# Expert weight rows relaid over partitions so that each partition reads 8 KB in one piece, in a hybrid decoder layer

## The reference

```python
# h: (256, 1024); 32 experts, each token uses 2 of them (gates is zero elsewhere)
def expert(acc, prm):
    wg, wu, wd, gt = prm                     # (1024, 512), (1024, 512), (512, 1024), (256,)
    hid = jax.nn.silu(h @ wg) * (h @ wu)
    return acc + gt[:, None] * (hid @ wd), None
out, _ = lax.scan(expert, jnp.zeros_like(h), (w_gate, w_up, w_down, gates.T))
```

## Time and profile before

| | us |
|---|---|
| median of 3 runs | 739.86 |
| lowest, highest of them | 738.91, 739.90 |
| span of the profiled execution | 794.1 |

### The profile page before, as it was taken

How to read it: one execution, slowest core, us unless ns; L and a number is a source line. 1 busy time by engine, 2 the same in 40 slices (tenths; PEclk the granted TensorE clock), 3 DMA queues, 4 the chain that set the end, 5 groups by cost and what they waited for, 6 DMA issues and landing times.

```text
span 794.1 us, 13163 instructions
## 1 busy us (share of the span) xinstructions
PE 771.8 (97%) x4865; PEld 590.9 (74%) x4865; DVE 647.9 (82%) x579; ACT 524.6 (66%) x577; POOL 139.2 (18%) x190
## 2 busy tenths in 40 slices
PE   6999999999799999999999999999999999999994
PEld 6774774535688888888888888888888888888873
DVE  3631759656869999999899999999899999999895
ACT  4011333544577888787887888787887888787883
POOL 5400200130231122111111122111111122111000
PEclk9988888888788888888888888888888888888887
DMA  9998966943598999999999999999999999999901
GB/s 320 352 369 319 386 241 253 360 170 118 188 321 307 357 359 352 343 355 349 358 343 355 372 343 359 335 358 359 355 335 363 349 359 352 342 358 357 323 1 56
DMA packets 102153, 249.20 MB, mean 314 GB/s; under 512 B 5265, under 2 KB 5325, under 8 KB 100077
## 3 DMA queue, kind: packets, MB, share of 16 engines
q1 hardware_dynamic: 99648, 244.33, 84.9%
q0 software_dynamic: 1008, 3.31, 1.2%
q10 hardware_dynamic: 1470, 1.22, 0.5%
HBM read 247.78 MB, written 1.07 MB: 313 GB/s over the span
## 4 chain that ended last, share of the span: by engine, by line
PE 95%; DVE 2%; DMA 1%; ACT 1%; issue 0%; SPq 0%; DVEq 0%
PE PS L1558 48%; PE PS L1546 8%; PE PS L1507 6%; PE PS L1252 4%; PE PS L1296 4%; PE PS L1525 4%; PE PS L1516 4%; PE PS L1413 3%; PE PS L1308 2%; PE PS L1290 2%; DMA W<-in_w_ada_dram 1%; PE PS L1180 1%; PE PS L1451 1%; PE PS L1325 1%; PE PS L1205 1%; PE PS L1337 1%
## 5 line engine op out<-in xcount | busy, mean ns | idle before, releaser
L1092 DVE TENSOR_TENSOR WL<-W,WH 128x2048 fp32r<-128x2048 f32 x185 | 417.8, 2298 | 36.1 <-ACT WH L711 36.1
L711 ACT CAST WH<-W 128x2048 fp32r<-128x2048 f32 x185 | 346.4, 1907 | 0.0
L1558 PE MATMUL PS<-WH,XT 128*128 128x512 f32 x512 | 152.3, 422 | 1.4 <-DVE XT L1111 1.4
L1558 PE MATMUL PS<-WL,XT 128*128 128x512 f32 x508 | 148.5, 417 | 0.0
L1558 PEld LDWEIGHTS PS<-WL,XT 128*128 128x128 f32 x508 | 97.5, 192 | 30.0
L1558 PEld LDWEIGHTS PS<-WH,XT 128*128 128x128 f32 x512 | 96.7, 195 | 26.6 <-DVE XT L1111 1.5
L458 POOL COPY cur<-PG 128x2 f32 (+1 forms) x31 | 5.7, 184 | 410.0 <-PE PS L1536 409.6
L1558 PE MATMUL PS<-WH,HT 128*128 128x512 f32 x248 | 72.6, 417 | 0.5 <-issue 0.5
L1558 PE MATMUL PS<-WL,HT 128*128 128x512 f32 x248 | 72.5, 417 | 0.0
L1558 PEld LDWEIGHTS PS<-WH,HT 128*128 128x128 f32 x248 | 47.3, 191 | 15.2 <-issue 0.6
L1558 PEld LDWEIGHTS PS<-WL,HT 128*128 128x128 f32 x248 | 47.9, 193 | 14.4
(11 more groups left out here) (242 smaller groups left out, 922.7 us busy)
## 6 DMA issues: line engine op xcount, KB each, us to landing
W<-in_w_gate_dram SPq DMA_DIRECT2D x64, 1024.0 KB, 8.1
W<-in_w_down_dram SPq DMA_DIRECT2D x64, 1024.0 KB, 5.7
W<-in_w_up_dram SPq DMA_DIRECT2D x63, 1024.0 KB, 9.0
W<-in_w_ada_dram SPq DMA_DIRECT2D x16, 1024.0 KB, 7.8
W<-in_w_in_dram SPq DMA_DIRECT2D x12, 1024.0 KB, 7.5
W<-in_w_ada_dram SPq DMA_DIRECT2D x16, 512.0 KB, 5.3
W<-in_w_out_dram SPq DMA_DIRECT2D x4, 1024.0 KB, 7.3
toe<-line_dram POOLq DMA_DIRECT2D x1, 1536.0 KB, 10.7
```

The lines of the kernel that those rows point to most:

```text
L711: nc.scalar.copy(WH[(UPE * odd + u) % SPLITS][:], source).then_inc(hi_ready, 1)
L1092: nc.vector.tensor_tensor(low, source, WH[(UPE * odd + u) % SPLITS][:].bitcast(f32), ALU.subtract).then_inc(lo_ready, 1)
L1558: last = nc.tensor.matmul(PS[:, bank, :], lhsT, w[:, q * 512:(q + 1) * 512], start=begin, stop=end)
```

## The change

`unit_source` gives partition p the rows `h*512 + 4*p` to `h*512 + 4*p + 3` of a gate or up matrix (rows `h*256 + 2*p` and `+ 1` of a down matrix), which lie behind one another in memory: 8 KB in one piece. A unit is now one piece of 1 MB. The gather and the turning steps take every fourth or every second column, so that the features come in the same order. The view of the spare unit's target (`Hn`) is reshaped to fit. Nothing else changes: number, order and size of all instructions and DMAs, waits and buffers stay.

```diff
             if u < 4:
                 w = (w_gate, w_up)[u // 2]
-                v = w.rearrange("l e (h k p) f -> h (l e) p k f", p=P, h=2)[u % 2]
+                v = w.rearrange("l e (h p k) f -> h (l e) p (k f)", p=P, h=2)[u % 2]
             else:
-                v = w_down.rearrange("l e (h k p) f -> h (l e) p k f", p=P, h=2)[u - 4]
-            return v[bass.ds(e, 1)].rearrange("a p k f -> p (a k) f")
+                v = w_down.rearrange("l e (h p k) f -> h (l e) p (k f)", p=P, h=2)[u - 4]
+            return v[bass.ds(e, 1)].rearrange("a p f -> p a f")
...
-                    sp.dma_start(Hn[:].rearrange("p t (two f) -> p (t two) f", two=2), unit_source(SPARE // UPE, SPARE % UPE)).then_inc(spare_in, 16)
+                    sp.dma_start(Hn[:].rearrange("p t f -> p (t f)").rearrange("p (o f) -> p o f", o=1), unit_source(SPARE // UPE, SPARE % UPE)).then_inc(spare_in, 16)
...
                     for k in range(DC):
+                        first = k // 4 * FF + k % 4
                         for t in range(TT):
                             for part in range(3):
-                                last = nc.tensor.matmul(PS[:, 2, k * SLOTS:(k + 1) * SLOTS], H3[:, part, t, k * P:(k + 1) * P],
+                                last = nc.tensor.matmul(PS[:, 2, k * SLOTS:(k + 1) * SLOTS], H3[:, part, t, first:first + FF - 3:4],
...
                     for q in range(FC):
-                        last = nc.tensor.matmul(PS[:, 0, q * SLOTS:(q + 1) * SLOTS], GU[:, q * P:(q + 1) * P], stack2[:],
+                        first = q // 2 * 2 * P + q % 2
+                        last = nc.tensor.matmul(PS[:, 0, q * SLOTS:(q + 1) * SLOTS], GU[:, first:first + 2 * P - 1:2], stack2[:],
                                                 start=True, stop=True)
...
# the same two lines in transpose_up, for q in range(FC, 2 * FC)
```

## The result

The changed kernel takes 746.06 us (median of 4 runs, 745.30 to 746.39) against 739.38 us for the kernel before (4 runs, 737.73 to 739.90). The ratio is 1.0094 with a 95% interval of 1.0077 to 1.0112: slower by 0.9%, 6.7 us.

A forecast was written before the change was run, and what follows sets the result against it. The prediction took DVE (16.63 us per period) to bound the timed runs, ahead of DMA (15.8) and PE (15.2). Loads, gather and turning summed to 0 on 739.86, written as 739.5 us; range 731 to 757, the forecast's own 737 to 742.

The forecast's parts named there:

- The clock of the timed runs: Whole kernel: timed runs (739.86 us) taken to have a higher PE clock than the profiled 794.1 us span, upper level 1.00.
- DVE's wait for `XT`: DVE's wait in each expert's period, 0.19 us, in a chain through ACT; predicted to stay at the upper clock.
- the one for `WH`: DVE's wait for ACT's `WH`, 1.18 us per period; predicted to go when PE is early.
- PE 17.84 x 0.85 = 15.2 us: PE's time per expert period at the upper clock, scaled from the profile; put PE third behind DVE and DMA.
- rival C: PE's gather and turning: weight loads with a step slower, 2.5 us per expert at profiled clock, about 764 us; chance 0.12 in full.
- gather alone slower: 742: PE's gather loads only slower, 0.6 us per expert, mostly hidden by DVE: 742 us; chance 0.14 including other partial prices.
- The two terms set to 0: PE's gather with a step of four columns and turning products with a step of two: each predicted to cost 0.
- The other rule of the Trainium skill: PE's weight loads: non-FP32 weights read 32 bits at a time, so the gather's step-of-four loads take twice as long.
- The loads: DMA weight loads in 8 KB pieces: 14.7 us per period in place of 15.8, worth 0 while DVE is the bound.
- the sign that I named for it: DMA loads: gate and up units landing in 7 us or less, against 8.1 and 9.0 before.
- Rival B: DMA loads bound the timed runs after all; gain 31 x 0.17 = 5 us, to 734.6 us; chance 0.20.
- Rival D: DMA: long pieces cut again into small packets, nothing changes, time as forecast; chance 0.54 together with the forecast.

## Why the prediction was wrong

The range of 731 to 757 us held the time, but the forecast was no change, with a chance of 0.25 for slower. By its steps:

**The clock of the timed runs** was inferred rightly: executions profiled at 1.00 take as long as the timed ones, 1.7 to 1.9 us more than their spans. So was the period before, 16.63 us, though for the wrong reason. The prediction added DVE's wait for `XT` to its busy time and let the one for `WH` go. At the full clock it is the other way round: in the 28 periods of the kernel before, the only thing that DVE waits for is `WH`, 8.6 us in all and 0.31 per period.

```profile
DVE WL L1092 <- ACT WH L711: 8.6, 29, 0.4
```

DVE alone needs 16.2, and the 16.63 come from the loop through PE, ACT and DVE, which no row of an execution with PE as the bound shows. That the two numbers agree is chance.

**The step that failed is "PE 17.84 x 0.85 = 15.2 us".** It scaled all of PE's time by the clock. Measured at the full clock: 56 big products (scatter included) 13.13 us without the loop's 0.10, in place of 14.20 x 0.85 = 12.07, turning 1.76 in place of 1.62, gather 1.42 in place of 1.30. That is 1.32 us more, and PE's length comes out at 16.54. The hint stood in the prediction itself: it called the turning products load-bound, and what a load bounds doesn't go with the columns. For the big products the rows gave no hint, since the first profile has them only at 0.85 or less; at 0.85 they took exactly what the clock gives, and their other limit, 232 ns, lay hidden below 251.

**So the point from which rival C decides was not 1.4 us per expert but 0.10.** C's place was right, its mechanism right, its price far too high: 0.21 us for the gather (0.6 worked out at the profiled clock, 5.4 as the upper end) and 0.09 for turning (1.9). C with a seventh of its price gave the result, because the slack was a fourteenth of what I had. The form "gather alone slower: 742" comes out at 743.9 measured.

**The two terms set to 0 were not 0.** Gather and turning cost 0.21 and 0.09 us. By these sums it took both faults for the miss: with 1.4 us of slack these prices would have shown only at the first experts, about 1 us, and with 0 for both the thin slack would have cost nothing. I took them from the rule of the Trainium skill (Advanced Engine Details and Errata, SBUF Cachelines), by which two hits in a line of 16 bytes suffice. The run with the change has two hits and a load of 118 ns for 98: here the measurement differs and decides. The other rule of the Trainium skill that was weighed (TensorE: Matmul & The Clock Gate, Weight-path perf modes — Fast Weight Load (FWL) and DoubleRow), as the prediction read it, would make a step of two cost as a step of four; step 2 is free (98 ns), so it isn't that either. By either rule steps of 4 and of 8 bytes would cost the same, and the measured price begins between them.

**The loads** were judged rightly: 44,809 packets, nothing gained. Only the sign that I named for it was wrong: gate and up units land in 7.9 and 8.7 us and not in 7 or less. SP issues two units together, so that a unit's landing may include its neighbour's; no run tests this.

**Rival B** is out: the layout alone is at 1.0001. **Rival D** is out by the packets.

## What to carry to other kernels

A profile at a lower clock than the timed runs can hide limits that aren't PE's clock: what looked like 1.4 us of slack after scaling was 0.1 here, so each kind of product must be asked whether columns or loads or a fixed rate bound it, and where the answer is open, slack should be taken as none. When two limits lie within 1% of each other (here a loop at 16.63 and PE at 16.54), small prices don't add: each edit alone costs its price less the slack, and only all of them together show the full one. A relayout for longer DMA pieces pays only where somebody waits for loads; before making PE pay for it, read whether any engine does.

## What the runs showed of the hardware

- Weight loads of 128 bfloat16 columns: 98 ns dense and with a step of 4 bytes, 118 ns at 8, 175 ns at 16; products of 64 columns then follow at 29.6, 34 and 63 ns. With float32 and a step of 8 bytes the turning products go from 0.84 and 0.92 to 0.88 and 0.97 us per eight records.
- Products of float32r take 0.447 ns per column at the full clock, 232 ns for 512, and 251 at 0.85; records of plain float32 with 256 columns take 216 and 251 ns and so go with the clock.
- With float32 read from SBUF at a step of 16 bytes, ACT takes about twice as long (1.04 to 2.04 us) and DVE 1.6 times (L1004, 1.22 to 1.99), while ACT reads PSUM with a step of 8 bytes as fast as dense (0.587 us both ways).
